# State-space scan: the third tile's weights amid the gate's projection, and the state's part scaled on ScalarE head by head

## What is computed

```python
def step(state, inp):
    x_c, dt_c, b_c, c_c = inp
    acs = jnp.cumsum(dt_c * a, axis=1)
    seg = acs[:, :, None] - acs[:, None, :]
    decay = jnp.exp(jnp.where(causal, seg, -jnp.inf))
    cb = jnp.einsum('bign,bjgn->bijg', c_c, b_c)
    w = cb[..., None] * decay * dt_c[:, None]
    y_diag = jnp.einsum('bijgr,bjgrp->bigrp', w, x_c)
    y_off = jnp.einsum('bign,bgrpn->bigrp', c_c, state) * jnp.exp(acs)[..., None]
    ...
y = y + d_skip * xs
y = rmsnorm_2(y * jax.nn.silu(z), gate_norm_w, SSM_NORM_EPS)
return jnp.einsum('ble,ed->bld', y, w_out)
```

## Time and profile before

| | us |
|---|---|
| median of 3 runs | 1827.02 |
| lowest and highest | 1826.83, 1827.07 |
| the profiled execution | 1826.83 |
| its span | 1825.2 |
| scan, from its first output to the first matmul of the output projection | 774.8 to 809.5 |

### The profile page before, as it was taken

The page is one execution under the profiler, slowest core; times in us unless marked ns, Lnnn a source line. Parts: engine busy times, 40 slices in busy tenths (PEclk is TensorE's granted clock), DMA queues, the critical chain, the costliest instruction groups (busy, mean ns, idle before and its releaser), DMA issues.

```text
span 1825.2 us, 26918 instructions
## 1 busy us (share of the span) xinstructions
PE 1807.5 (99%) x9194; PEld 1530.7 (84%) x9194; DVE 1499.7 (82%) x1856; ACT 1266.0 (69%) x1660; POOL 138.2 (8%) x230
## 2 busy tenths in 40 slices
PE   9999999999999999999999999999999999999998
PEld 7888888888888899888888888888888888888886
DVE  6686777778656788585999998999999999999998
ACT  5645565556445566666878778787787777877876
POOL 2040050000000000140230000000000000000100
PEclk9999999999999999999999999999999999999999
DMA  9424469554555455515899999999999999999994
GB/s 331 157 96 139 166 193 341 190 200 144 185 187 183 160 187 185 176 39 179 322 376 402 404 373 378 394 349 413 376 368 391 361 402 377 369 401 373 377 413 176
DMA packets 239644, 512.48 MB, mean 281 GB/s; under 512 B 11036, under 2 KB 58490, under 8 KB 239498
## 3 DMA queue, kind: packets, MB, share of 16 engines
q1 hardware_dynamic: 235634, 493.08, 74.1%
q0 software_dynamic: 3808, 18.38, 2.5%
q10 hardware_dynamic: 144, 0.26, 0.0%
HBM read 505.38 MB, written 12.07 MB: 284 GB/s over the span
## 4 chain that ended last, share of the span: by engine, by line
PE 94%; DVE 3%; ACT 1%; issue 1%; DMA 0%; POOL 0%; SPq 0%; DVEq 0%; ACTq 0%; POOLq 0%
PE ps L262 25%; PE ps L264 25%; PE ps L263 25%; PE ps L2565 9%; PE ps L2568 4%; PE ps L2840 1%; DVE w_lo L255 1%; PE ps L2360 1%; PE ps L2723 1%; PE ps L2818 0%; DMA raw<-in_w_in_dram 0%; PE ps L2283 0%; PE ps L2304 0%; PE ps L2680 0%; ACT w_hi L246 0%
## 5 line engine op out<-in xcount | busy, mean ns | idle before, releaser
L255 DVE TENSOR_TENSOR w_lo<-raw,w_hi 128x1024 fp32r<-128x1024 f32 x938 | 1105.1, 1227 | 127.0 <-ACT w_hi L246 126.4
L246 ACT ACTIVATE w_hi<-raw 128x1024 fp32r<-128x1024 f32 x938 | 942.0, 1055 | 241.7 <-PE ps L264 229.5
L262 PE MATMUL ps<-w_hi,a 128*128 128x512 f32 (+1 forms) x1216 | 480.6, 395 | 2.0 <-DVE w_lo L255 0.9
L264 PE MATMUL ps<-w_hi,a 128*128 128x512 f32 (+1 forms) x1216 | 472.8, 389 | 0.0
L263 PE MATMUL ps<-w_lo,a 128*128 128x512 f32 (+1 forms) x1216 | 471.8, 388 | 0.0
L262 PE MATMUL ps<-w_hi,a_hi 128*128 128x512 f32 (+1 forms) x720 | 280.7, 390 | 0.9 <-DVE arena L1607 0.4
L264 PE MATMUL ps<-w_hi,a_lo 128*128 128x512 f32 (+1 forms) x720 | 278.7, 387 | 0.0
L263 PE MATMUL ps<-w_lo,a_hi 128*128 128x512 f32 (+1 forms) x720 | 278.6, 387 | 0.0
L262 PEld LDWEIGHTS ps<-w_hi,a 128*128 128x128 f32 x1216 | 228.5, 188 | 49.1 <-issue 1.7
L264 PEld LDWEIGHTS ps<-w_hi,a 128*128 128x128 f32 x1216 | 228.2, 188 | 47.9
L263 PEld LDWEIGHTS ps<-w_lo,a 128*128 128x128 f32 x1216 | 228.6, 188 | 44.2
(11 more groups left out here) (395 smaller groups left out, 1442.2 us busy)
## 6 DMA issues: line engine op xcount, KB each, us to landing
raw<-in_moe_w_gate_dram SPq DMA_DIRECT2D x112, 1024.0 KB, 7.2
raw<-in_moe_w_up_dram SPq DMA_DIRECT2D x112, 1024.0 KB, 7.6
raw<-in_moe_w_down_dram SPq DMA_DIRECT2D x112, 1024.0 KB, 7.0
raw<-in_ssd_w_in_dram SPq DMA_DIRECT2D x24, 1024.0 KB, 5.0
raw<-in_w_ffn_in_dram SPq DMA_DIRECT2D x22, 1024.0 KB, 5.0
raw<-in_w_in_dram SPq DMA_DIRECT2D x21, 1024.0 KB, 6.6
raw<-in_w_ffn_out_dram SPq DMA_DIRECT2D x11, 1024.0 KB, 4.9
raw<-in_dense_w_gate_dram SPq DMA_DIRECT2D x11, 1024.0 KB, 5.1
```

What stands on the lines that cost most here:

```text
L246: nc.scalar.activation(w_hi[:, u % SPL, part], raw[:, u % RAW, part], ACT.Copy).then_inc(hi_done, 1)
L255: last = nc.vector.tensor_tensor(w_lo[:, u % SPL, part], raw[:, u % RAW, part], w_hi[:, u % SPL, part].bitcast(F32), ALU.subtract)
L262: nc.tensor.matmul(o, lh, rh, start=start, stop=False, skip_group_check=True)
L264: return nc.tensor.matmul(o, ll, rh, start=False, stop=stop, skip_group_check=True)
```

## The change

The weights of tile 2 are taken out of the loop on TensorE, ScalarE and VectorE. TensorE does them between the two halves of the gate's last quarter. ScalarE does `decays(2)` ahead of `z_out(3)`. VectorE does `weights(2)` ahead of the loop, and waits there for three quarters of the gate instead of four; the fourth is waited for at k = 12. L1918 is gone from VectorE: ScalarE's `state_part(k)` waits for the tile's output and scales ps[7] in place, with four Copy activations of 128x64, each with a head's `eacs` as its scale per partition. It stands after `decays(k + 2)`, for k = 1 ahead of it. VectorE waits for `act_scaled` ahead of L1923, and at k = 1 accumulates ahead of `weights(3)`. The semaphore `sd_ex` becomes `act_scaled`. The first unit of the output projection (`first_out`) does the left halves of both token tiles first, into banks ps[4] and ps[6], after `st_acc` 15, and the right halves, into ps[5] and ps[7], after `st_acc` 16; the same 24 matmuls in another order.

```diff
--- before.py
+++ after.py
@@ -582,7 +582,7 @@
         low, high = slice(0, 512), slice(512, D)
 
         sd_raw, sd_T, st_gate = sem("sd_raw"), sem("sd_T"), sem("st_gate")
-        sd_y, sd_l, sd_dta, sd_acs, sd_te, sd_ex = (sem("sd_" + k) for k in ("y", "l", "dta", "acs", "te", "ex"))
+        sd_y, sd_l, sd_dta, sd_acs, sd_te, act_scaled = (sem(k) for k in ("sd_y", "sd_l", "sd_dta", "sd_acs", "sd_te", "act_scaled"))
         c_vec, c_tap, c_one, c_two, c_conv, c_silu = (sem("c_" + k) for k in ("vec", "tap", "one", "two", "conv", "silu"))
         xt_ps, xt_act, xt_dve, zs_done = sem("xt_ps"), sem("xt_act"), sem("xt_dve"), sem("zs_done")
         st_skip, st_xd, st_seg, st_ex, st_w, st_y, st_s, st_sc, st_acc = (
@@ -690,7 +690,7 @@
                 pool.dma_start(result_rows.rearrange("(i p) d -> i p d", p=P),
                                bcast(token_rows[S:S + P, :], 0, MAX_TASKS)).then_inc(y_out, 16)
                 pool.wait_ge(sd_dta, 1)
-                pool.wait_ge(sd_ex, 1)
+                pool.wait_ge(act_scaled, 1)
                 pool.wait_ge(xt_act, 5)
                 pool.wait_ge(xt_dve, 5)
                 pool.wait_ge(s_rowv, 64)
@@ -1227,7 +1227,7 @@
 
                 act.wait_ge(sd_te, 1)
                 nc.scalar.activation(eacs, acs, ACT.Exp)
-                nc.scalar.activation(tend, tend, ACT.Exp).then_inc(sd_ex, 1)
+                nc.scalar.activation(tend, tend, ACT.Exp).then_inc(act_scaled, 1)
                 for r in range(0, 10, 2):
                     act.wait_ge(xt_ps, r + 1)
                     nc.scalar.activation(xt_dst(r), ps[r % 4][:, :], ACT.Copy).then_inc(xt_act, 1)
@@ -1254,17 +1254,31 @@
                     split_hi(act, Z0 + 2 * b + 3)
                     split_hi(act, Z0 + 2 * b + 4)
                     z_out(b)
+                def state_part(k):
+
+                    act.wait_ge(st_y, k + 1)
+                    for r in range(HPG):
+                        hd = NH + HPG * (k // 2) + r
+                        part = ps[7][:, r * HD:(r + 1) * HD]
+                        last = nc.scalar.activation(part, part, ACT.Copy, scale=eacs[:, hd:hd + 1])
+                    last.then_inc(act_scaled, 1)
+
                 decays(0)
                 decays(1)
                 split_hi(act, O0 + 1)
+                decays(2)
                 z_out(3)
                 for k in range(2 * NG):
                     if k % 2 == 0:
                         act.wait_ge(st_s, k // 2 + 1)
                         nc.scalar.activation(s_st, ps[6][:, 0:256].rearrange("p (r e) -> p r e", r=HPG),
                                              ACT.Copy).then_inc(st_sc, 1)
-                    if k + 2 < 2 * NG:
+                    if k == 1:
+                        state_part(k)
+                    if 2 < k + 2 < 2 * NG:
                         decays(k + 2)
+                    if k % 2 and k > 1:
+                        state_part(k)
                 turn_gain_act(act, "y", chunks_two(a0_hi, a1_hi), DC, lambda c: V_GN + c)
                 split_hi(act, O0 + 2)
                 split_hi(act, O0 + 3)
@@ -1904,22 +1918,20 @@
                     nc.vector.tensor_copy(xt_dst(r), ps[r % 4][:, :]).then_inc(xt_dve, 1)
                 for u in range(3, 9):
                     split_lo(dve, Z0 + u)
-                dve.wait_ge(sd_ex, 1)
+                dve.wait_ge(act_scaled, 1)
 
                 def accumulate(k):
 
                     g, t = k // 2, k % 2
-                    heads = slice(t * NH + HPG * g, t * NH + HPG * (g + 1))
                     xv = xs[:, t, g * 256:(g + 1) * 256].rearrange("p (r e) -> p r e", r=HPG)
                     dve.wait_ge(st_y, k + 1)
                     dve.wait_ge(st_skip, k + 1)
                     before = ps[7][:, 0:256].rearrange("p (r e) -> p r e", r=HPG)
-                    if t:
-                        nc.vector.tensor_tensor(before, before, bcast(eacs[:, heads], 2, HD), ALU.mult)
                     last = nc.vector.tensor_tensor(xv, xv, ps[4 + k % 2][:, 0:256].rearrange("p (r e) -> p r e", r=HPG),
                                                    ALU.add)
                     if t:
                         C.link(last)
+                        dve.wait_ge(act_scaled, g + 2)
                         last = nc.vector.tensor_tensor(xv, xv, before, ALU.add)
                     last.then_inc(st_acc, 1)
                     dve.wait_ge(st_acc, k + 1)
@@ -1936,13 +1948,19 @@
                 weights(0)
                 weights(1)
                 split_lo(dve, O0 + 1)
-                dve.wait_ge(zs_done, 4)
+                weights(2)
+                dve.wait_ge(zs_done, 3)
                 for k in range(2 * NG):
                     if k == 2 * NG - 1:
                         turn_gain_dve(dve, "y", chunks_two(a0_hi, a1_hi), chunks_two(a0_lo, a1_lo), 2, lambda c: V_GN + c)
-                    if k + 2 < 2 * NG:
+                    if k == 12:
+                        dve.wait_ge(zs_done, 4)
+                    if k == 1:
+                        accumulate(1)
+                    if 2 < k + 2 < 2 * NG:
                         weights(k + 2)
-                    accumulate(k)
+                    if k != 1:
+                        accumulate(k)
                 turn_gain_dve(dve, "y", chunks_two(a0_hi, a1_hi), chunks_two(a0_lo, a1_lo), DC, lambda c: V_GN + c, 2)
                 split_lo(dve, O0 + 2)
                 split_lo(dve, O0 + 3)
@@ -2727,12 +2745,14 @@
                 tile_weights(0)
                 tile_weights(1)
                 pe.wait_ge(zs_done, 2)
-                mm_rows(pe, Z0 + 6, ps[6:8])
+                mm_rows(pe, Z0 + 6, ps[6:8], halves=(0,))
+                tile_weights(2)
+                mm_rows(pe, Z0 + 6, ps[6:8], halves=(1,))
                 pe.wait_ge(zs_done, 3)
                 for k in range(2 * NG):
                     if k and k % 2 == 0:
                         tile_state(k // 2)
-                    if k + 2 < 2 * NG:
+                    if 2 < k + 2 < 2 * NG:
                         tile_weights(k + 2)
                     tile_output(k)
                     if k == 0:
@@ -2756,7 +2776,20 @@
                     for b in range(2):
                         turn_router(0, b)
 
-                pe.wait_ge(st_acc, 2 * NG)
+
+                def first_out():
+
+                    u, slot = O0, O0 % SPL
+                    pe.wait_ge(lo_done, u + 1)
+                    for half in range(2):
+                        pe.wait_ge(st_acc, 2 * NG - 1 + half)
+                        for k in range(2):
+                            cols = slice(k * D + half * 512, k * D + (half + 1) * 512)
+                            for t in range(T):
+                                mm = mm3(ps[4 + 2 * t + half][:, :], a0_hi[:, k, t * P:(t + 1) * P], a0_lo[:, k, t * P:(t + 1) * P],
+                                         w_hi[:, slot, cols], w_lo[:, slot, cols], k == 0, False)
+                    mm.then_inc(unit_used, 1)
+
                 for k in range(8):
                     if k == 2:
                         pe.wait_ge(st_gate, 2 * NG)
@@ -2764,8 +2797,10 @@
                     pe.wait_ge(turn_lo, 2 * (TURN["y"] + k + 1))
                     hi, lo = (a0_hi, a0_lo) if k < 4 else (a1_hi, a1_lo)
                     at = slice(2 * (k % 4), 2 * (k % 4) + 2)
-                    if k < 7:
-                        mm_down(pe, O0 + k, hi[:, at], lo[:, at], ps[4:8], k == 0, False)
+                    if k == 0:
+                        first_out()
+                    elif k < 7:
+                        mm_down(pe, O0 + k, hi[:, at], lo[:, at], ps[4:8], False, False)
                     else:
                         mm_down_end(pe, (O0 + k,), hi[:, at], lo[:, at], ps[4:8],
                                     middle=turn_first if level >= 5 else None)
```

## The result

| | before | after |
|---|---|---|
| median | 1827.04 us (19 runs) | 1829.84 us (19 runs) |
| lowest to highest | 1826.83 to 1827.90 | 1828.24 to 1832.66 |
| the profiled execution, its span | 1826.83, 1825.2 | 1829.01, 1827.3 |

The ratio of after to before is 1.0016, with a 95% interval of 1.0010 to 1.0022: 2.8 us more, which lies within the 0.2% that I counted as no change, and in the range on record. The profiled execution is 2.2 us above that of before. The spread has grown too: 4.4 us from the lowest to the highest run, against 1.1. Nine of the 19 runs lie at 1828.24 to 1829.57, all with a mean clock of 0.999; the other ten lie at 1829.84 to 1832.66, nine of them with 0.996 to 0.998. The median is the cheapest of these ten.

The account below looks back on a forecast made before the run. TensorE, busy for all 4.02 us of a group, was taken to bound the kernel. Losses of 1.25 at the start and 0.6 at the end gave +1.9 us, a median of 1828.9; range 1826.4 to 1830.8, leaving out the clock.

Parts of the forecast that it names:

- TensorE bounds the scan: Steady scan: TensorE is busy for all 4.02 us of a group, so relieving VectorE is worth nothing and the period stays.
- Part 1, the state product 0.54 later: Start: with tile 2's weights amid the gate, its last matmul ends 0.69 later; first state starts at 776.2 instead of 775.66.
- Part 2, the exchange and the stall at tile 5: Start, k = 1: table exchange follows tile 1's scaling (0.93); TensorE stalls 2.5 us at tile 5; start loses 1.25.
- The rival in which the compiler hides the exchange: Table load put ahead of the scaling at k = 1; tile 5's stall shrinks by 1.28: +0.6, 1827.6; 15 in 100.
- A rule against it: ScalarE's table switch also costs a drain of about 1.38 us: sum 3.3, median 1830.3; 2 in 100.
- Part 4, the end: Output projection: first splits stand behind the last scaling, low parts come after it; start at 811.4, the end loses 0.6 us.
- The sum: Start's loss of 1.25 and end's loss of 0.6: projection starts at 811.4 instead of 809.52, +1.9 us.
- the clock: Rival: the stall at tile 5 might bring TensorE from 2.4 to 1.2 GHz: 1830.9 to 1832.8; 8 in 100.
- The median: Whole kernel: 1828.7 for the profiled execution, median 0.2 above it, so 1828.9; 62 in 100.
- half to a whole group at half speed: Price of a clock fall after the stall at tile 5: 2 to 4 us on top of 1.9.
- my own signs of being wrong: Among them: clock under 1.00, period other than 4.02, ScalarE idle under 0.3 us a group, projection starting before 810.

## Why the prediction was right, and which term it left out

- *TensorE bounds the scan.* Right for the steady part. Its period stayed 4.02 with VectorE at 3.54 and ScalarE at 3.45. But "moving work off another engine wins nothing by itself" was too broad. Placed well, the move is worth some 0.6 us: 0.34 in the first groups, which the prediction did not see, and 0.24 at the end, of which it had counted 0.19. In the change itself the order at both ends hid this.
- *Part 1, the state product 0.54 later* (776.2 against 775.66). It begins 1.33 after the first output (776.55 and 775.22) instead of 0.84: 0.5. Right.
- *Part 2, the exchange and the stall at tile 5.* Stated 2.5 us, found 2.52 in the queue (783.65 against 780.32 + 0.81), 2.33 of it idle; the loss at the start 1.25 stated, 1.28 found. The rival in which the compiler hides the exchange fell: it stands at 780.28, behind the scaling. The price of the scaling was 0.93 stated, 0.90 found. That the order at k = 1 is the cause, and nothing else of the move, is shown by the run that reverses it.
- *A rule against it.* Scaling to 780.26, load at 780.28, Exp at 781.58: 1.30 us. There is no room in it for the drain of about 1.38 us that the Trainium skill (ScalarE: Activation LUTs, section What ACT_TABLE_LOAD costs) adds to each switch. The measurement decides; the chain would otherwise have given a stall of 3.7.
- *Part 4, the end.* 0.6 lost stated, 0.5 found. The low parts are the later of the two, as said; the run with the splits moved shows it, and that the new first unit pays 0.84 where they are not.
- *The sum.* +1.9 stated. With the clock kept up by dummy work +1.83, and +1.9 for the nine cheap runs of the change (median 1828.93 against 1827.04). The traces have 1.28 + 0.5.
- *The median.* +1.9 stated, +2.8 found. The term that was mis-sized is the clock. I had it as a rival at 8 in 100, in which a run would cost 2 to 4 us more. In fact it happened in 7 of 11 runs of the changed kernel on one chip, judged by their times, at 1.65 us in the traced one, and so belongs to the median itself. The price of "half to a whole group at half speed" was somewhat too high, the chance far too low: the wait of 2.5 us that I had computed myself was longer than the 1.7 us after which the clock had fallen at the end of the program, and I played that row down because the end had thin work ahead of it. The scan, with all of TensorE's time taken ahead of its wait, fell as well. The condition that I set was wrong too: "it decides if the fall comes before TensorE resumes". In all four falls that were traced behind a wait the clock dropped only as TensorE resumed or up to 1.5 us after it, even behind 4.17 us of standing still, and it still cost its 1.6. A clock under 1.00, one of my own signs of being wrong, was seen. (The Trainium skill, TensorE: Matmul & The Clock Gate, section Why this matters for your kernels, warns of idle stretches in the middle of a kernel; the trace agrees, with windows at 0.60 and 0.54 behind one of 2.33 us.)

Of the 2.8 us: 1.28 at the start, 0.5 at the end, and about 1.0 for the clock, the difference that the dummy work makes to the median. That the median stayed inside a range which left the clock out is partly luck: it depends on how many executions have the fall, and on its price being 1.65 and not 2 to 4. Three of the 19 runs (1831.66, 1831.71 and 1832.66, mean clock 0.996) lie 2.7 to 3.7 above the cheap ones, more than one fall of 1.65. No trace shows such a run, so whether the clock fell twice in it is open.

## What to carry to other kernels

When a step is moved ahead of another on an engine that works in order, follow the one it is put in front of: here a scaling of 0.9 us that waits for the newest result stood ahead of work that was ready, and took a table exchange of 1.28 us along into the open. A wait of TensorE of over 2 us, as here, should be priced with the clock behind it, as a chance and not as a certainty: runs that fall into two clusters hint at it, and the granted clock by windows shows whether and where it fell. A wider spread alone does not show it. And where one engine is exhausted (TensorE at 4.02 of 4.02), relief of another is worth nothing in the steady part; look for it at the two ends. There the early weights, the reordered unit and the scaling in its right place were worth 2.4 us together.

## What the runs showed of the hardware

- Nine useless matmuls in a wait made the program faster by 1.0 us in the median (1829.15 against 1830.18); the granted clock, 0.60 and 0.54 behind the wait without them, read 1.00 with them.
- After a wait of 2.2 to 2.3 us the clock fell in some executions and not in others of one and the same program (7 of 11, and 6 of 11, judged by their times); after one of 4.2 us in all six; after one of 1.28 or 1.41 us in none of the traces. In the four falls that were traced behind such waits the clock dropped 0 to 1.5 us after the work had resumed, not in the wait, and was back at the upper level 3.4 to 4.9 us after it had resumed. The price was 1.65 and 1.63 us in the two traces where it was worked out.
- An Exp table exchange took 1.28 us and the next activation began 0.02 us later.
- Four scalings of 128x64 on ScalarE from PSUM to PSUM took 0.90 us, a single one 0.29 (median of 32).
- VectorE's multiplication by the gate (L1927, both operands in SBUF) takes 0.42 us in 11 of the 16 tiles of before, and 0.87 to 0.89 in the five where a GpSimd operation had started 0.01 to 0.02 us ahead of it (794.31 behind 794.29, for one).
